# Up products of the second block's feed-forward by Strassen's scheme, with late roots of four norms and a final norm in two halves

## The chip, the cores and the metric

The kernel runs on one core of one Trainium2 chip. The metric is the device time of the whole program, 3941.75 us as the median of 3 runs (3941.59 to 3943.38). TensorE (PE) multiplies, VectorE (DVE) and ScalarE (ACT) do arithmetic on 128 partitions, GpSimd (POOL) so far only starts transfers, and SyncE (SP) loads the weights.

## The reference

Two blocks of two layers each work on 512 tokens of 1024 features. The first block is a gated linear attention layer and a latent attention layer, each with a convolutional feed-forward. The second block, twice over, is: a root-mean-square norm, three attentions side by side (a chunk band, a differential one, and one whose keys an indexer picks), a gated mix, a cross attention, and a SwiGLU feed-forward. A final norm ends it. What the change touches:

```python
def rmsnorm_2(x, g):
    x32 = x.astype(jnp.float32)
    y = x32 * lax.rsqrt(jnp.mean(x32 * x32, axis=-1, keepdims=True) + EPS)
    return y.astype(x.dtype) * g

# in each layer of the second block
h = rmsnorm_2(x, norm_mix)      # its first products: the indexer's queries and keys
...
h = rmsnorm_2(x, norm_ffn)
gate, up = split(h @ w_gu, 2)   # 1024 -> 2 x 2816
x = x + (silu(gate) * up) @ w_down
# after both layers
return rmsnorm_2(x, final_norm)
```

The last function stands here in short form. All is float32.

## The kernel before

Activations lie with features on the partitions: X is 8 tiles (k or n) of 128 features by tokens. Each float32 operand is split into a high part rounded to the matmul's 32-bit format (by ACT) and the rest (by DVE), and each product is three matmuls, high by high, high by low, low by high (mms3). MH and ML are the two parts of the normed activations, WH and WL those of a weight piece.

Weight pieces come in the order of one list through a ring of four slots (SP). Two pairs WH, WL take turns: piece k+1 is split while PE works on piece k, and the split waits until the products of piece k-1 are done. split_act and split_dve do this, and the code that calls them sets the place in each engine's queue. Every queue is in order, and semaphores join them.

The feed-forward of the second block (ffn_pe, swiglu_act, swiglu_dve, down_pe, down_act, down_dve; tags b0 and b1) goes over 22 column tiles j of the 2816 hidden features: j = 0 alone, then seven groups of three. A group has three up steps, each with a gate and a value product of 8 x 3 matmuls of 512 tokens. After a group's up steps come the down products of the group before, in two weight pieces (called D0 and D1 here) of four output tiles each. Between, ACT takes the silu of the gate, DVE multiplies by the value (called hidden here), and the result is split again into IH and IL (inter).

A norm (adaln, square_act, square_sum_dve, mean_pe, hr_act, hnorm_act, hnorm_dve) squares each finished tile of X on ACT, sums tiles 0 to 5 on DVE, and has PE multiply by a matrix of 1/1024 three times (the sum, tile 6 and tile 7), which leaves the mean on all partitions. ACT then makes the root by Ln and Exp, DVE scales each tile by root and gain, ACT rounds it to MH, DVE makes ML. The first product after a norm takes tile k as soon as it is there (first_mms3). Six such norms stand in the second block; the change touches those called "m" (before the indexer) and "f" (before the feed-forward) of both layers, and the final one.

Of the kernel before, what the change touches and what calls it, by code (L numbers as in the profile page):

```python
# [29 lines left out]
P = 128  # L30
# [80 lines left out]
def build(nc, io, counts):  # L111
    known = counts.known
    ctx = ExitStack()
    with ctx:
# [45 lines left out]
        conv = overlay("conv", [P, 2, 2, TOK], F32, 2 * HALF + 2 * inter_words)  # L160
        ps = ctx.enter_context(nc.psum_tensor("ps", [P, 8, BANK], F32))
# [29 lines left out]
        dve_done = ctx.enter_context(nc.semaphore("dve_done"))  # L191
        slot_loaded = [ctx.enter_context(nc.semaphore(f"slot_loaded_{i}")) for i in range(SLOTS)]
# [143 lines left out]
        splits = []  # L336
        for i, (key, parts, split) in enumerate(plan):
            loads[i % SLOTS] += 16 * len(parts)
            where[key] = (i, loads[i % SLOTS])
            if split:  # L340
                splits.append(key)
        split_at = {key: k for k, key in enumerate(splits)}

# [55 lines left out]

        def split_act(k):  # L400
# [3 lines left out]
            key = splits[k]  # L404
            i, n = where[key]
# [5 lines left out]
        def split_dve(k):  # L411
# [3 lines left out]
            key = splits[k]  # L415
            nc.vector.wait_ge(act_done, at(("rounded", k)))
# [17 lines left out]
        turn = [0]  # L434

        def take(key, bank=None):

            if bank is None:
                bank = turn[0] % 6
                turn[0] += 1  # L440
# [116 lines left out]
        def norm_buffers(spec):  # L557
            return late_tiles if spec[0] == "n0f" else (NF, NR)

        def residual_tiles(spec):  # L560
# [3 lines left out]
            if key == "n1":  # L564
                halves = (range(4), range(4, DT))
                return [(n, t0, tn) for (t0, tn), half in zip((ALL[0], ALL[1], ALL[1], ALL[0]), (0, 0, 1, 1)) for n in halves[half]]
            return [(n, t0, tn) for n in range(DT) for t0, tn in groups]

        def norm_tiles(groups):
            return [(k, t0, tn) for t0, tn in reversed(groups) for k in range(DT)]  # L570

# [12 lines left out]
        def square_act(spec, i):  # L584
# [4 lines left out]
            if i >= 2 and summed_squares(spec)[i - 1]:  # L589
                nc.scalar.wait_ge(dve_done, at(("hsq_summed", key, i - 1)))  # L590
# [7 lines left out]
        def square_sum_dve(spec, i):  # L598

            if i < 0 or not summed_squares(spec)[i]:  # L600
# [6 lines left out]

        def mean_pe(spec, i):
# [5 lines left out]
            n, t0, tn = tiles[i]  # L614
            bank = 7 if t0 else 6
            first = min(j for j in range(len(tiles)) if tiles[j][1] == t0 and own_product(spec, j))
            if i == first:
                take(("hms", key, t0), bank)
            if summed_squares(spec)[i]:
                nc.tensor.wait_ge(dve_done, at(("hsq_summed", key, i)))  # L620
            else:
                nc.tensor.wait_ge(act_done, at(("hsq", key, i)))
            m = nc.tensor.matmul(ps[:, bank, 0:tn], mat("mean1024"), NSQ[:, i % 2, 0:tn], start=(i == first), stop=(n == DT - 1))  # L623
            m.then_inc(pe_done, mark("pe", ("hsq_read", key, i), ("hms", key, t0)))
# [10 lines left out]
        def hnorm_act(spec, between=lambda i: None):  # L635
            key, groups, gains, shifts = spec
            for t0, tn in reversed(groups):
                hr_act(spec, t0, tn)
                for i, (k, u0, un) in enumerate(norm_tiles(groups)):
                    if u0 == t0:  # L640
                        nc.scalar.wait_ge(dve_done, at(("hscaled", key, i)))
                        nc.scalar.activation(hs(k, t0, tn, groups is MAIN)[0], norm_buffers(spec)[0][:, i % 3, 0:tn], ACT.Identity,
                                             bias=shifts(k, 0 if t0 else 1) if shifts else 0.0).then_inc(
                                                 act_done, mark("act", ("hh", key, i)))
                        between(i)

        GAINS = {"n0f": (0, 1), "n1": (1, 0), "n1f": (1, 1)}

        def hnorm_dve(spec, between=lambda i: None):
            key, groups, gains, shifts = spec  # L650
            tiles = norm_tiles(groups)
# [3 lines left out]
            def rest(i):  # L655
                k, t0, tn = tiles[i]
                nc.vector.wait_ge(act_done, at(("hh", key, i)))
                f = norm_buffers(spec)[0][:, i % 3, 0:tn]
# [8 lines left out]
            for i, (k, t0, tn) in enumerate(tiles):  # L667
# [7 lines left out]
                nc.vector.scalar_tensor_tensor(norm_buffers(spec)[0][:, i % 3, 0:tn], X[:, k, t0:t0 + tn], gains(k, 0 if t0 else 1),  # L675
                                               norm_buffers(spec)[1][:, t0:t0 + tn], ALU.mult, ALU.mult).then_inc(
                                                   dve_done, mark("dve", ("hscaled", key, i)))
# [94 lines left out]
        def residual_pe(key, act_in, groups, spec, chunks=None, passes=None):  # L772

            done = 0
            for name, tokens in passes or [(key, groups)]:
                for ck, n0, nn in chunks or [((name, i), 2 * i, 2) for i in range(DT // 2)]:
                    w = weights(ck)
                    kt = w.shape[1]
                    for j in range(nn):
                        for t0, tn in tokens:  # L780
# [4 lines left out]
                            if done > MEAN_LAG:  # L785
                                mean_pe(spec, done - 1 - MEAN_LAG)
# [2689 lines left out]
```

## Time and profile before

| what | value |
|---|---|
| median of 3 runs | 3941.75 us |
| profiled execution, its own time | 3945.47 us |
| its span | 3943.7 us |
| PE busy | 3759.4 us (95%) |
| DVE busy | 2040.9 us (52%) |
| ACT busy | 1423.2 us (36%) |
| POOL busy | 57.9 us (1%) |
| granted clock of TensorE, mean | 0.99 |

The span is what the trace covers, some 1.8 us less than the execution's time. A matmul's row has the time until its result is out; the next starts long before that, so the pace of PE is the distance from start to start. The first feed-forward of the second block runs from 2529 to 2893 us, the second from 3567 to 3931 us.

### The profile page before, as it was taken

Reading aid. Unit: us, or ns where it says so; the run is one execution under the profiler, and the core shown is the slowest. Engines: PE = TensorE matmul, PEld = TensorE weight load, DVE = VectorE, ACT = ScalarE, POOL = GpSimd, SP = SyncE. Lnnn points to the kernel's source line nnn. Section 1 sums busy time; section 2 is a strip of 40 time slices with the busy share of each in tenths; the row PEclk is TensorE's granted clock in tenths of the full one; section 3 lists DMA queues with packets and bytes.
Section 4 is the critical chain, followed back from the end, with each engine's and each line's share of the span. In section 5 each row is a group of like instructions: output and inputs, shape, how many; then the busy total and the mean of one; then the engine's idle time right before and its main releaser. Section 6 shows DMA issues by size and latency. Waiting matters only on the chain.

```text
span 3943.7 us, 48507 instructions
## 1 busy us (share of the span) xinstructions
PE 3759.4 (95%) x19650; PEld 2928.2 (74%) x19650; DVE 2040.9 (52%) x3190; ACT 1423.2 (36%) x2340; POOL 57.9 (1%) x115
## 2 busy tenths in 40 slices
PE   7998999999989899999999999899999999999998
PEld 6776888888855557887767677688876666867887
DVE  4553454454533326556786544443368765344334
ACT  4323332222344423333344443422234445433222
POOL 0000000000000000000000000000000000000000
PEclk9999999999999999999999999999999999999999
DMA  6321434233210012332322032233332222322331
GB/s 213 99 80 50 152 100 129 91 114 101 76 39 20 25 56 83 97 96 88 109 89 84 29 108 90 67 105 98 94 111 75 78 65 75 107 75 86 96 98 62
DMA packets 394091, 346.14 MB, mean 88 GB/s; under 512 B 11984, under 2 KB 355536, under 8 KB 393744
## 3 DMA queue, kind: packets, MB, share of 16 engines
q1 hardware_dynamic: 386912, 321.71, 26.8%
q0 software_dynamic: 6960, 21.34, 1.9%
q8 instruction: 158, 2.59, 0.3%
q14 instruction: 61, 0.50, 0.0%
HBM read 330.96 MB, written 2.10 MB: 84 GB/s over the span
## 4 chain that ended last, share of the span: by engine, by line
PE 78%; DVE 9%; ACT 4%; issue 2%; DMA 0%; POOL 0%; ACTq 0%; DVEq 0%
PE ps L455 51%; PE ps L466 4%; PE ps L468 4%; PE ps L467 4%; DVE WL L417 2%; PE ps L2384 1%; PE ps L2362 1%; PE ps L1971 1%; PE ps L1984 1%; ACT WH L409 1%; DVE arena_m L2635 1%; PE ps L695 1%; PE ps L623 1%; PE ps L696 1%; PE ps L697 1%
## 5 line engine op out<-in xcount | busy, mean ns | idle before, releaser
L417 DVE TENSOR_TENSOR WL<-ring,WH 128x2048 fp32r<-128x2048 f32 (+4 forms) x245 | 498.0, 2033 | 367.1 <-ACT WH L409 366.7
L409 ACT CAST WH<-ring 128x2048 fp32r<-128x2048 f32 (+4 forms) x245 | 415.5, 1696 | 431.6 <-PE ps L455 314.0
L455 PE MATMUL ps<-MH,WH 128*128 128x512 f32 (+1 forms) x1024 | 400.0, 391 | 8.1 <-DVE WL L417 8.1
L455 PE MATMUL ps<-ML,WH 128*128 128x512 f32 (+1 forms) x1024 | 399.8, 390 | 0.0
L455 PE MATMUL ps<-MH,WL 128*128 128x512 f32 (+1 forms) x1024 | 399.8, 390 | 0.0
L455 PE MATMUL ps<-IH,WH 128*128 128x512 f32 (+1 forms) x880 | 327.7, 372 | 7.7 <-DVE modv L756 3.2
L455 PE MATMUL ps<-IL,WH 128*128 128x512 f32 (+1 forms) x880 | 324.9, 369 | 0.0
L455 PE MATMUL ps<-IH,WL 128*128 128x512 f32 (+1 forms) x880 | 324.2, 368 | 0.0
L466 PE MATMUL ps<-MH,WH 128*128 128x512 f32 x768 | 321.6, 419 | 0.0
L468 PE MATMUL ps<-MH,WL 128*128 128x512 f32 x768 | 301.4, 392 | 0.0
L467 PE MATMUL ps<-ML,WH 128*128 128x512 f32 x768 | 300.2, 391 | 0.0
L455 PE MATMUL ps<-HH,WH 128*128 128x512 f32 (+1 forms) x728 | 247.3, 340 | 1.4 <-DVE WL L417 1.4
L455 PE MATMUL ps<-HL,WH 128*128 128x512 f32 (+1 forms) x728 | 245.5, 337 | 0.0
L455 PE MATMUL ps<-HH,WL 128*128 128x512 f32 (+1 forms) x728 | 245.0, 336 | 0.0
L455 PEld LDWEIGHTS ps<-MH,WH 128*128 128x128 f32 (+1 forms) x1024 | 192.3, 188 | 50.8 <-DVE WL L417 9.8
L455 PEld LDWEIGHTS ps<-MH,WL 128*128 128x128 f32 (+1 forms) x1024 | 192.2, 188 | 41.2
L455 PEld LDWEIGHTS ps<-ML,WH 128*128 128x128 f32 (+1 forms) x1024 | 192.1, 188 | 40.7
L1596 ACT ACTIVATE conv<-ps,vec 128x512 f32<-128x512 f32 (+1 forms) x132 | 92.4, 706 | 322.8 <-PE ps L455 322.1
L1616 DVE SCALAR_TENSOR_TENSOR conv<-ps,vec,conv 128x511 f32<-128x511 f32 (+1 forms) x132 | 86.9, 658 | 216.2 <-ACT conv L1596 215.7
L455 PEld LDWEIGHTS ps<-IH,WH 128*128 128x128 f32 x880 | 166.3, 189 | 39.4 <-DVE WL L417 4.4
L466 PEld LDWEIGHTS ps<-MH,WH 128*128 128x128 f32 x768 | 144.5, 188 | 60.3 <-DVE arena_m L2016 9.7
L455 PEld LDWEIGHTS ps<-IH,WL 128*128 128x128 f32 x880 | 166.2, 189 | 28.2
(338 smaller groups left out, 6782.8 us busy)
## 6 DMA issues: line engine op xcount, KB each, us to landing
ring<-in_w_in SPq DMA_DIRECT2D x62, 1024.0 KB, 5.2
ring<-in_w_ada SPq DMA_DIRECT2D x48, 1024.0 KB, 8.0
ring<-in_ffn_w_up SPq DMA_DIRECT2D x88, 512.0 KB, 5.1
ring<-in_w_gu SPq DMA_DIRECT2D x88, 512.0 KB, 5.0
ring<-in_ffn_w_down SPq DMA_DIRECT2D x28, 768.0 KB, 4.8
ring<-in_w_down SPq DMA_DIRECT2D x28, 768.0 KB, 4.4
ring<-in_gla_w_in SPq DMA_DIRECT2D x24, 512.0 KB, 3.9
arena_m<-arena_m POOLq DMA_DIRECT2D x72, 128.0 KB, 2.9
```

Of the source, the lines that this page charges most:

```text
L409: nc.scalar.copy(split_slot(key, WH), raw_slot(key)).then_inc(act_done, mark("act", ("rounded", k)))
L417: nc.vector.tensor_tensor(split_slot(key, WL), raw_slot(key), split_slot(key, WH).bitcast(F32), ALU.subtract).then_inc(dve_done, mark("dve ...
L455: m = nc.tensor.matmul(out, l, r, start=(i == 0), stop=(i == len(pairs) - 1))
L466: nc.tensor.matmul(out, lh, rh, start=first and i == 0, stop=False)
L467: nc.tensor.matmul(out, lh, rl, start=False, stop=False)
L468: m = nc.tensor.matmul(out, ll, rh, start=False, stop=end)
L623: m = nc.tensor.matmul(ps[:, bank, 0:tn], mat("mean1024"), NSQ[:, i % 2, 0:tn], start=(i == first), stop=(n == DT - 1))
L695: nc.tensor.matmul(out, wh, xh, start=(k == 0), stop=False)
L696: nc.tensor.matmul(out, wl, xh, start=False, stop=False)
L697: m = nc.tensor.matmul(out, wh, xl, start=False, stop=(k == DT - 1))
L1596: nc.scalar.activation(conv[:, j % 2, part, t0:t0 + tn], bank_of(key)[:, 0:tn], ACT.Identity, scale=v("conv_w", 132 * l + 44 + t), bias=v( ...
L1616: nc.vector.scalar_tensor_tensor(cv[:, t0 + 1:t0 + tn], u[:, 0:tn - 1], v("conv_w", 132 * l + t), cv[:, t0 + 1:t0 + tn], ALU.mult, ALU.add ...
```

## The change

**Seven products for eight.** For the column tiles j = 4 to 21 of b0 and b1, the up step (K = 1024, 256 output columns, 512 tokens) is cut into 2 x 2 blocks: K in halves of 4 tiles, columns in gate and value, tokens in halves of 256. Seven products p1 to p7 of 4 x 3 matmuls of 256 tokens stand for the 48 matmuls of 512. The weight blocks are four parts of the slot (a11, a12, a22, and s1 in place of a21) and three sums s2, s3, s4, which GpSimd makes. Each of the seven is split on its own ("chunk"), in two turns of the pair WH, WL. The token sums are made once per layer (XF, split into TH and TL). The results are put together on ACT (p1, p5, p7 copied from PSUM), GpSimd (u4, u3, c22) and DVE (q, c11, c12, c21).

**Late roots.** Before the norms m and f, the first product runs on x times gain, not yet times the root; its result is multiplied by the root afterwards (raw_scaled_dve). The normed tiles are still made, for the next products. The sums of squares move from DVE to GpSimd.

**Final norm in halves.** The last four output tiles of the last down step are made for tokens 256 to 511 first, then for 0 to 255; root, scaling and store go by halves.

```diff
+        def seven(key):
+            return key[0] == "up" and key[1][0] == "b" and key[2] >= FIRST_SEVEN
...
+        CHUNKS = (("a11", "s2", "s1", "s3"), ("a12", "s4", "a22"))
...
+        def chunk_act(k, c):
...
+            if last[0] == "seven" and c < len(CHUNKS[last[2]]):
+                nc.scalar.wait_ge(pe_done, at(("chunk_used", k - SPLITS, c)))
+            else:
+                nc.scalar.wait_ge(pe_done, at(("split_used", k - SPLITS)))
...
+            nc.scalar.copy(chunk_place(k, c, WH), chunk_source(key, name)).then_inc(
+                act_done, mark("act", ("chunk_rounded", k, c)))
...
+        def combine_pool(key, name, before):
+            out, a, b, op = {"s3": ("s3", "a11", "a21", ALU.subtract), "s1": ("s1", "a21", "a22", ALU.add),
+                             "s2": ("s2", "s1", "a11", ALU.subtract), "s4": ("s4", "a12", "s2", ALU.subtract)}[name]
...
+            if before and name != "s1":
+                nc.gpsimd.wait_ge(dve_done, at(("chunk_of", before, name)))
...
+        def raw_mms3(spec, tiles):
+            key = spec[0]
+            for k in range(DT):
+                nc.tensor.wait_ge(dve_done, at(("raw_low", key, k)))
+                for out, w, t0, tn in tiles:
...
+                if k < RAW_MEANS:
+                    mean_pe(spec, DT - RAW_MEANS + k)
...
         def hnorm_dve(spec, between=lambda i: None):
             key, groups, gains, shifts = spec
+            if raw(spec):
+                split_dve(after(first_piece(spec)))
...
+                    if spec[0][0] == "m" and i == 4:
+                        split_dve(after(("idx", spec[0][1], 1)))
...
+        PRODUCTS = [("p1", 0, 0, "a", FIRST_HALF, (MH, ML), 0, FIRST_HALF), ("p6", 0, 1, "a", SECOND_HALF, (TH, TL), QUARTER, SECOND_HALF),
+                    ("p5", 0, 2, "b", FIRST_HALF, (TH, TL), 0, FIRST_HALF), ("p7", 0, 3, "b", SECOND_HALF, (TH, TL), 0, SECOND_HALF),
+                    ("p2", 1, 0, "c", FIRST_HALF, (MH, ML), QUARTER, FIRST_HALF), ("p3", 1, 1, "c", SECOND_HALF, (MH, ML), QUARTER, SECOND_HALF),
+                    ("p4", 1, 2, "d", FIRST_HALF, (TH, TL), QUARTER, FIRST_HALF)]
...
+        def seven_dve(tag, j):
...
+            nc.vector.wait_ge(pe_done, at(("p3", tag, j)))
+            add_bank(gate[:, FIRST_HALF], "c", FIRST_HALF, gate[:, FIRST_HALF], "c11")
+            nc.vector.wait_ge(pool_done, at(("u4", tag, j)))
+            add_bank(gate[:, SECOND_HALF], "c", SECOND_HALF, gate[:, SECOND_HALF], "c12", ("free", ("seven", tag, j, "c")))
+            if nxt:
+                chunk_dve(nxt + 1, 1)
+            else:
+                split_dve(after(key))
...
+        def combined_low_dve(tag, part):
+            ks = slice(QUARTER * part, QUARTER * part + QUARTER)
+            nc.vector.wait_ge(act_done, at(("combined_high", tag, part)))
+            nc.vector.tensor_tensor(TL[:, ks, :], XF[:, ks, :], TH[:, ks, :].bitcast(F32), ALU.subtract).then_inc(
+                dve_done, mark("dve", ("combined_low", tag, part)))
...
+            combined_inputs_pool(tag)
+            combine(0)
+            combine(1)
+            for n, key in enumerate(keys):
...
+                for name, dst, a, b in (("u4", gate[:, SECOND_HALF], q, value[:, SECOND_HALF]),
+                                        ("u3", value[:, FIRST_HALF], value[:, FIRST_HALF], q),
+                                        ("c22", value[:, SECOND_HALF], value[:, SECOND_HALF], value[:, FIRST_HALF])):
...
+                combine(n + 2)
...
+            if spec[0] == "final" and g == GROUPS - 1:
+                tiles = residual_tiles(spec)
+                return [(tiles[k][0] // 4, [(n % 4, t0, tn) for n, t0, tn in tiles[k:k + 4]]) for k in range(0, 12, 4)]
...
-            nc.vector.wait_ge(act_done, at(("hr", "final", CTX)))
-            for k in range(DT):
+        def final_dve(half, ks):
+            t0, tn = FINAL_HALVES[half]
+            for k in ks:
+                nc.vector.wait_ge(act_done, at(("hr", "final", t0)))
```

DVE's queue at the last up step of a group in b0 and the down step behind it, before (conv holds gate and value):

```order
L417 TENSOR_TENSOR WL<-ring,WH 128x1536 [waits act_done]
L1649 TENSOR_TENSOR conv<-ps,conv 128x512 [waits act_done,pe_done]
L1582 TENSOR_TENSOR IL<-conv,IH 128x512 [waits act_done]
L417 TENSOR_TENSOR WL<-ring,WH 128x1536 [waits act_done]
L1672 TENSOR_TENSOR X<-ps,X 128x512 [waits dve_done,pe_done] x4
```

The same place of the changed kernel (TB holds gate and value; q, c11, c12, then the split, then c21):

```order
L1835 TENSOR_TENSOR TB<-ps,TB 128x256 [waits act_done]
L1835 TENSOR_TENSOR TB<-ps,TB 128x256 [waits pe_done]
L1835 TENSOR_TENSOR TB<-ps,TB 128x256 [waits pool_done]
L502 TENSOR_TENSOR WL<-ring,WH 128x1536 [waits act_done]
L1835 TENSOR_TENSOR TB<-ps,TB 128x256 [waits pool_done,pe_done]
L1863 TENSOR_TENSOR TB<-TB 128x512 [waits dve_done,act_done]
L1940 TENSOR_TENSOR ILB<-TB,IHB 128x512 [waits act_done]
L502 TENSOR_TENSOR WL<-ring,WH 128x1536 [waits act_done]
L2057 TENSOR_TENSOR X<-ps,X 128x512 [waits dve_done,pe_done] x4
```

The split of D0 stood first, and waited for ACT alone; now it stands behind c11 and c12, of which the first waits for p3, the last product but one of the step.

DVE's queue in b0 from the normed tile 7 to the down step of j = 0, in the changed kernel (L761 multiplies by the root, L2023 and L2028 are hidden, L1889 the rest of the token sums):

```order
L835 TENSOR_TENSOR ML<-XF,MH 128x512 [waits act_done] x2
L761 TENSOR_TENSOR TB<-ps,spare 128x512 [waits pe_done] x2
L2023 TENSOR_TENSOR TB<-TB 128x512 [waits act_done,dve_done]
L1940 TENSOR_TENSOR ILB<-TB,IHB 128x512 [waits act_done]
L502 TENSOR_TENSOR WL<-ring,WH 128x2048 [waits act_done]
L2028 TENSOR_TENSOR TB<-ps,TB 128x512 [waits act_done,pe_done]
L1940 TENSOR_TENSOR ILB<-TB,IHB 128x512 [waits act_done]
L502 TENSOR_TENSOR WL<-ring,WH 128x2048 [waits act_done]
L2028 TENSOR_TENSOR TB<-ps,TB 128x512 [waits act_done,pe_done]
L1940 TENSOR_TENSOR ILB<-TB,IHB 128x512 [waits act_done]
L1889 TENSOR_TENSOR TL<-XF,TH 128x2048 [waits act_done]
L502 TENSOR_TENSOR WL<-ring,WH 128x512 [waits act_done]
```

Before, the split for j = 1 stood where the two L761 stand; it has moved ahead of the normed tiles. L761 and L1889 were not there.

GpSimd's queue in the changed kernel behind the token sums, where before there was nothing (the four sums of one weight piece, the three additions of one step, the next sums):

```order
L474 TENSOR_TENSOR SB<-ring 128x512 [waits dve_done,slot_loaded_1]
L474 TENSOR_TENSOR ring<-ring 128x4x128 [waits pool_done]
L474 TENSOR_TENSOR SB<-ring 128x512 [waits dve_done,pool_done]
L474 TENSOR_TENSOR SB<-ring,SB 128x512 [waits dve_done,pool_done]
L1914 TENSOR_TENSOR TB<-TB 128x256 [waits dve_done,act_done]
L1914 TENSOR_TENSOR TB<-TB 128x256
L1914 TENSOR_TENSOR TB<-TB 128x256 [waits pool_done]
L474 TENSOR_TENSOR SB<-ring 128x512 [waits dve_done,slot_loaded_2]
```

The sums for a piece two steps ahead stand behind the additions of the present step, and wait for the split of the piece between.

## Rows read from the trace of the kernel before

**Rows 1.** The page: span, busy time, and the chain's shares by engine.
```profile
span 3943.7 us, 48507 instructions
PE 3759.4 (95%) x19650; PEld 2928.2 (74%) x19650; DVE 2040.9 (52%) x3190; ACT 1423.2 (36%) x2340; POOL 57.9 (1%) x115
PE 78%; DVE 9%; ACT 4%; issue 2%; DMA 0%; POOL 0%; ACTq 0%; DVEq 0%
```

**Rows 2.** Stretches: length, busy of PE, PEld, DVE, ACT, POOL, clock, DMA.
```profile
1852.99:1890.03 37.04, 33.34 (x127) 24.10 (x125) 18.55 (x21) 14.88 (x21) 6.64 (x13) 0.91 0.59 174
2528.00:2534.50 6.50, 5.05 (x12) 4.01 (x13) 6.47 (x11) 3.74 (x6) 0.00 (x0) 0.50 0.06 22
2575.57:2583.09 7.52, 5.94 (x26) 4.24 (x24) 6.63 (x9) 4.55 (x4) 0.00 (x0) 1.00 0.33 105
2632.20:2664.84 32.64, 32.64 (x145) 27.04 (x144) 9.80 (x8) 8.13 (x8) 0.00 (x0) 1.00 0.36 98
2664.84:2681.16 16.32, 16.32 (x73) 13.52 (x72) 9.91 (x11) 3.91 (x3) 0.00 (x0) 1.00 0.29 95
2893.33:2929.13 35.80, 32.10 (x127) 23.24 (x125) 18.50 (x21) 14.82 (x21) 6.64 (x13) 0.95 0.62 180
```

**Rows 3.** Timeline of PE: first of 36 matmuls of 256 tokens, and what follows.
```profile
1051.02 0.28 PE L455 MATMUL ps<-IH,WH 128*128 128x256 f32 x1
...
1055.33 0.40 PE L455 MATMUL ps<-IH,WH 128*128 128x512 f32 x1
```

**Rows 4.** Groups by line and shape, 2529 to 2893 us: busy, mean ns, idle.
```profile
L417 DVE TENSOR_TENSOR WL<-ring,WH 128x1536 fp32r<-128x1536 f32 x14 | 24.6, 1758 | 9.9 <-ACT WH L409 9.9
L409 ACT CAST WH<-ring 128x1536 fp32r<-128x1536 f32 x14 | 20.7, 1475 | 12.1 <-PE ps L455 12.1
L417 DVE TENSOR_TENSOR WL<-ring,WH 128x2048 fp32r<-128x2048 f32 x21 | 48.1, 2291 | 22.5 <-ACT WH L409 22.5
L409 ACT CAST WH<-ring 128x2048 fp32r<-128x2048 f32 x22 | 41.9, 1903 | 60.2 <-PE ps L455 60.2
L417 DVE TENSOR_TENSOR WL<-ring,WH 128x512 fp32r<-128x512 f32 x2 | 1.4, 684 | 0.0
L409 ACT CAST WH<-ring 128x512 fp32r<-128x512 f32 x2 | 1.2, 615 | 0.0
```

**Rows 5.** Groups by line and shape, whole span: PSUM operands of 256 columns.
```profile
L2003 DVE TENSOR_TENSOR arena_m<-ps,arena_m 128x256 f32<-128x256 f32 x16 | 6.7, 421 | 0.3
L2035 ACT COPY arena_m<-ps 128x256 f32<-128x256 f32 x16 | 6.0, 373 | 28.9 <-PE ps L1971 28.9
```

**Rows 6.** Timeline at norm f of b0: start, us, engine, line, idle before.
```profile
2522.82 2.92 PE L623 MATMUL ps<-spare,mats 128*128 128x512 f32 x6
...
2525.79 0.69 ACT L630 ACTIVATE stage_b<-ps,eps 128x512 f32<-128x512 f32 x1 [1.22 <-PE ps L623]
...
2527.17 1.41 DVE L675 SCALAR_TENSOR_TENSOR stage_b<-X,vec,stage_b 128x512 f32<-128x512 f32 x2 [3.45 <-ACT stage_b L633]
...
2529.45 0.76 PE L695 MATMUL ps<-MH,WH 128*128 128x512 f32 x1 [3.70 <-DVE ML L664]
...
2536.21 1.47 DVE L664 TENSOR_TENSOR ML<-stage_b,MH 128x512 fp32r<-128x512 f32 x2
```

**Rows 7.** Timeline of the end: last means, final scaling, stores.
```profile
3930.80 2.92 PE L623 MATMUL ps<-spare,mats 128*128 128x512 f32 x6
...
3935.14 5.39 DVE L3252 SCALAR_TENSOR_TENSOR stage_b<-X,vec,stage_b 128x512 f32<-128x512 f32 x8 [3.45 <-ACT stage_b L633]
3936.59 4.31 SPq L3308 DMA_DIRECT2D out<-stage_b  x4
```

**Rows 8.** GpSimd's costliest group by line.
```profile
L2084 POOL DMA_DIRECT2D arena_m<-arena_m x80 | 38.9, 494 | 281.8 <-ACT arena_m L2040 238.1 <-DVE arena_m L2095 23.5 <-ACT arena_m L2575 7.6
```

**Rows 9.** Timeline of DVE: one split of 1024 columns.
```profile
3435.88 1.22 DVE L417 TENSOR_TENSOR WL<-ring,WH 128x1024 fp32r<-128x1024 f32 x1
```

More of the change, by code:

```diff
@@ L339, in build @@
             where[key] = (i, loads[i % SLOTS])
-            if split:
+            if seven(key):
+                for part in (0, 1):
+                    where["seven", key, part] = where[key]
+                    splits.append(("seven", key, part))
+            elif split:
                 splits.append(key)
         split_at = {key: k for k, key in enumerate(splits)}
+        for key in list(split_at):
+            if key[0] == "seven":
+                split_at[key[1]] = split_at["seven", key[1], 1]
         def after(key):
@@ L404, in split_act @@
             key = splits[k]
+            if key[0] == "seven":
+                for c in range(len(CHUNKS[key[2]])):
+                    chunk_act(k, c)
+                return
             i, n = where[key]
@@ L415, in split_dve @@
             key = splits[k]
+            if key[0] == "seven":
+                for c in range(len(CHUNKS[key[2]])):
+                    chunk_dve(k, c)
+                return
             nc.vector.wait_ge(act_done, at(("rounded", k)))
@@ L1517, in up_pe @@
             for j in group(g):
+                if seven(("up", tag, j)):
+                    seven_pe(tag, j)
+                    continue
                 w = split_weights(("up", tag, j))
-                if j == 0:
+                if j == 0 and raw(spec):
+                    tiles = [(take(("up", tag, j, part, CTX)), lambda k, part=part: two(w, k, 128 * part, 128 * part + 128), CTX, SEQ)
+                             for part in range(2)]
+                    raw_mms3(spec, tiles).then_inc(pe_done, mark("pe", ("raw_read", spec[0], DT - 1), ("up", tag, j, 0, CTX),
+                                                                 ("up", tag, j, 1, CTX), split_used(("up", tag, j))))
+                elif j == (1 if raw(spec) else 0):
                     for t0, tn in reversed(groups):
@@ L1547, in down_pe @@
                     out = take(("down", tag, g, 4 * i + n, t0))[:, 0:tn]
[L1548 to L1550 removed]
+                    m = mms3(out, [(two(w, k, 128 * n, 128 * n + 128), inter(tag, g, k, t0, t0 + tn)) for k in range(len(group(g)))])
                     m.then_inc(pe_done, mark("pe", ("down", tag, g, 4 * i + n, t0), ("down", tag, g),
@@ new lines, in seven_pe @@
+        def seven_pe(tag, j):
+            key = ("up", tag, j)
+            if j == FIRST_SEVEN:
+                nc.tensor.wait_ge(dve_done, at(("combined_low", tag, 1)))
+            for name, half, c, bank, part, (xh, xl), k0, tokens in PRODUCTS:
+                k = split_at["seven", key, half]
+                if part is FIRST_HALF:
+                    take(("seven", tag, j, bank))
+                out = bank_of(("seven", tag, j, bank))[:, part]
+                nc.tensor.wait_ge(dve_done, at(("chunk", k, c)))
+                wh, wl = chunk_place(k, c, WH), chunk_place(k, c, WL)
+                for i in range(QUARTER):
+                    nc.tensor.matmul(out, wh[:, i], xh[:, k0 + i, tokens], start=i == 0, stop=False)
+                    nc.tensor.matmul(out, wh[:, i], xl[:, k0 + i, tokens], start=False, stop=False)
+                    m = nc.tensor.matmul(out, wl[:, i], xh[:, k0 + i, tokens], start=False, stop=i == QUARTER - 1)
+                m.then_inc(pe_done, mark("pe", (name, tag, j), ("chunk_used", k, c), ("split_used", k)))
```

393 lines of the change are left out of this document (322 added, 71 removed).

## The prediction

> **What bounds the kernel now.** I read the page first, then stretches of the second block's feed-forward, then the timeline at the norms. PE is busy 95% of the span and carries 78% of the chain; DVE is at 52%, ACT at 36%, GpSimd at 1% [rows 1]. In a steady group the three up steps are 144 matmuls of 512 tokens in 32.64 us, the down step 72 in 16.32 us, both 0.2267 us apart with no gap, while DVE is busy 9.8 us of the 32.64 [rows 2]. So here only PE's pace counts. At a norm it is a chain: the last means start at 2522.82, the root takes until 2527.17, PE waits 3.70 us and starts again at 2529.45 [rows 6], and from 2528.0 to 2534.5 the granted clock is 0.50, the lower of its two levels (1.2 GHz), after that idle time [rows 2].
>
> **Fewer products.** Matmuls of 256 tokens run 36 in 4.31 us (1051.02 to 1055.33), 0.1197 us apart, each with a weight load of its own [rows 3]. That is 5.6% more than half of 0.2267, so not all of the eighth is gained. An up step goes from 48 x 0.2267 = 10.88 us to 84 x 0.1197 = 10.05 us, one product being 1.44 us: 0.83 us, times 18 steps, times 2 layers, **29.7 us less** if PE never waits.
>
> **What the seven products ask of the others.** Per up step DVE has seven chunk splits of 0.68 us [rows 4], four additions from PSUM of 0.42 us [rows 5], and hidden and inter of about 0.69: 7.9 us of 10.05. ACT has seven casts of 0.62 [rows 4], three copies of 0.37 [rows 5], silu and rounding of about 0.6 each: 6.7 us. Chunks for the next step follow the product that frees their place by one to three us, and PE needs them a whole step later, so in the first two steps of a group I see no wait. GpSimd does four sums of 512 columns and three of 256. No row shows it computing (it issues transfers, 0.49 us each) [rows 8]. From below I take DVE's time for the same shape, 0.68, from above DVE's for four times the columns, 2.29 [rows 4]: 4.0 to about 14 us per step. At the upper end GpSimd itself would bound the step. I take the lower half, near DVE's own time and under 1 us, and its sums then fit: they stand two steps ahead.
>
> **The last step of a group.** PE goes on with D0, whose weights DVE must have split. That split stood ahead of the step's work; now it stands behind c11, which waits for p3. Product p3 ends 8.62 us into the step, its result is out 0.2 us later, c11 and c12 take 0.35 us each from start to start, the split takes 1.76 [rows 4], and PE starts 0.15 us after it: 11.4 us, where p4 has ended at 10.05. PE waits 1.35 us in each group, six groups, two layers: **16.2 us more**. Behind the split wait c21, hidden, inter and the split of D1, and D1 is needed 8 us later: no second wait. The idle time is short; a like one of 1.5 us stands in 2575.57 to 2583.09, at full clock [rows 2].
>
> **Norm m (twice).** From the last down product the way to the end of the indexer's two pieces and the next 48 products took 37.04 us in the first layer and 35.80 in the second [rows 2]. Now the raw products start at once: 10.88 us and 2.6 us for three means, of which the third ends 6.65 us in. The root takes 1.6 us more, and the eight normed tiles go from 8.2 us at 1.27 us each (10.5 us from 2527.17 to 2537.68) [rows 6]. In their midst stands a split of 2048 columns, 1.90 us on ACT and 2.29 on DVE [rows 4], which puts the last tile at 22.4 us. PE, ready for the second piece at 13.5, takes tile after tile and ends it at 23.1 instead of 18.9; with 48 products, 34.0. **3.0 and 1.8 us less.**
>
> **Norm f (twice).** From the last product of the cross attention's output to the start of j = 4 it took 60.27 us (2522.82 to 2583.09) [rows 2, 6]. Now: 13.46 us of raw products and means, 10.88 for j = 1. DVE is through with the normed tiles at 18.75 us; then come two multiplications by the root, silu, hidden, rounding, inter, and the split for j = 2 ends at 25.8: PE waits 1.5 us. With j = 2 and 3 PE is at 47.6. At j = 3 DVE splits half of the token sums (1.90 us on ACT, 2.29 on DVE) [rows 4] ahead of the split of the second down piece, which is ready 6.7 us after the step instead of at 2.7; PE waits 4.0 us, and the first chunk comes behind four additions: 57.6. An idle time as long as the 3.70 us of before lets the clock fall. At norm m of the second layer 35.80 us [rows 2] less the 6.63 from last means to start [rows 6] leave 29.2 us for 120 matmuls, which at 0.2267 take 27.2: a fall costs 2.0 us. 59.6 against 60.27: **0.7 us less each.** The early idle time and clock are saved, and paid again 45 us later.
>
> **Final norm.** Half products cost 72 x 0.1197 - 36 x 0.2267 = 0.46 us, and five more means of half width 2.1 us ahead of the last product. Behind it the root and eight scalings are half as wide (8 x 0.67 = 5.39 us before) [rows 7], but DVE scales the first half in between, which puts the last addition back by 1.5 us. I make it 13.4 us from the old 3930.80, where it was 12.9: **0.5 us more**, give or take 1.5.
>
> **Sum.** 29.7 - 16.2 + 4.8 + 1.4 - 0.5 = 19.2 us. The profiled execution took 3945.47 us, 3.7 over the median of the runs: 3926.3 in such an execution, **3923 us** as the median, 0.5% less. Its own range is 3908 to 3937: GpSimd's sums and the waits at the norms may shift it by some 15 us either way.
>
> **Rivals.**
> First, slower: GpSimd and DVE hold each other up. Nothing in the trace shows the two computing at once [rows 8]. If no operation of GpSimd runs beside one of DVE with both inputs in SBUF, then the first two steps of a group have 21 splits and the like of DVE (14.4 us) and nine sums and six additions of GpSimd in one line. At DVE's own speed that is 8.7 us, 23.1 in all in 20.1 us and a slack of nearly 4: nothing happens. At half DVE's speed (1.22 us, the row of 1024 columns) [rows 9] it is 15.1 us and the middle step's inter ends 9.7 us into the last step instead of 4. ACT's cast for D0 stands behind it and ends at 11.3, DVE's split at 13.1: PE waits 3.2 us, not 1.35, and every second time the clock falls, 2.0 us. That is 12 x 4.2 = 50 us against 29.7. At norm f the token sums, four of 1024 columns at 2.29 us, would stand between hidden, inter and the split for j = 2: 4.0 us and a fallen clock more, in each layer. In all 27 us slower, **3969 us**. It decides from about 1 us per sum of 512 columns on. The Trainium skill states this lock (SBUF — State Buffer, section Who interferes with whom: a VectorE instruction with two SBUF inputs and a GpSimd instruction that reads SBUF block each other for the whole instruction). It also gives 4497 ns for a GpSimd addition of 2048 columns (GPSIMD Engine Reference, section 3.1), an estimate of 1.12 us for 512; with that and the lock the sum would come out near 3946, no gain. No run so far shows either.
>
> Second, better: DVE and ACT are quicker through these chains than I make them, GpSimd costs nothing, and the waits for D0 shrink to 0.7 us (8 us in all), those at f to half (4 us more): **3908 us**; without any such wait 3900.
>
> Third, the change does not do what it says: with a weight load for every 256 tokens instead of 512 PE's pace is that of the loads (84 instead of 48 per step). Loads take 0.19 us (27.04 for 144) but overlap [rows 2]; in 36 in a row they did not slow the pace [rows 3]. Were it 0.130 in the long run, a step would take 10.92 us and the 29.7 would be lost: **3953 us**.
>
> **Chances.** Forecast 0.48; GpSimd and DVE in each other's way 0.30, of which a third is the mild form near 3946; quicker chains 0.16; pace of loads 0.06. What a measurement of this kernel can tell from no change is about 0.2%, 8 us. Faster: the forecast but for its upper end, and the second rival, 0.61. Within 0.2%: the mild lock and small pieces of the others, 0.12. Slower: 0.27. The range from 3900 to 3972 leaves out the far ends of the first and second rival.
>
> **What would show it.** Right: L455-like rows of 256 tokens 0.120 us apart; PE idle some 1.1 to 1.4 us before each D0, released by DVE's split of 1536 columns, twelve times; no idle time between the cross attention's output and the raw products; 1.5 us before j = 2 and about 4 before the second down piece of j = 0, released by DVE. Wrong: DVE's splits of 512 columns at much over 0.69 us, or long idle times of DVE ended by GpSimd; GpSimd's sums over 1 us; waits for D0 over 3 us with the clock at 0.50 behind them; GpSimd busy through the whole up steps; or any wait of PE for a chunk.

## The result and the profile after

The changed kernel takes 3961.99 us as the median of 5 runs, against 3941.75 before: ratio 1.0047 (1.0036 to 1.0058), slower by 20.2 us by the medians (18.5 by the ratio), where 19 less was forecast. It lies 7 us below the first rival's 3969. The profiled execution took 3966.62 us, 21.1 more than that of before.

The page of the changed kernel, answering [rows 1]:

```profile
span 3964.8 us, 52752 instructions
PE 3748.3 (95%) x20992; PEld 2979.3 (75%) x20992; DVE 2314.5 (58%) x3586; ACT 1551.6 (39%) x2702; POOL 441.7 (11%) x395
PE 69%; DVE 15%; ACT 5%; issue 4%; POOL 0%; DMA 0%; ACTq 0%; DVEq 0%; POOLq 0%
L541 PE MATMUL ps<-IHB,WH 128*128 128x512 f32 (+1 forms) x364 | 146.0, 401 | 33.0 <-DVE WL L502 33.0
```

PE computes 11 us less than before, but DVE's share of the chain has grown from 9% to 15%: in front of the high-by-high down products (IHB, the rounded half of inter) PE stood idle 33.0 us, always released by DVE's split of a weight piece.

Stretches of the changed kernel, answering [rows 2]: norm m of the first layer, norm f, three up steps and the down step behind them, twice, and norm m of the second layer. Columns are length, then busy time of PE, PEld, DVE, ACT, POOL, the granted clock, DMA.

```profile
1854.01:1888.54 34.53, 31.72 (x126) 22.66 (x127) 20.63 (x26) 15.45 (x21) 7.76 (x14) 0.95 0.59 163
2521.09:2584.19 63.10, 55.09 (x225) 43.24 (x223) 41.86 (x44) 27.79 (x36) 18.58 (x9) 0.95 0.30 84
2638.11:2670.48 32.37, 30.40 (x254) 30.22 (x252) 28.67 (x34) 16.39 (x32) 23.56 (x18) 1.00 0.31 90
2670.48:2688.53 18.05, 18.05 (x72) 14.72 (x73) 10.60 (x15) 4.18 (x6) 4.21 (x4) 0.91 0.36 103
2688.53:2720.90 32.37, 30.39 (x253) 30.21 (x252) 28.68 (x34) 16.39 (x32) 23.56 (x18) 1.00 0.32 90
2720.90:2737.34 16.44, 16.44 (x72) 13.59 (x73) 10.50 (x15) 4.18 (x6) 4.22 (x4) 1.00 0.40 113
2901.65:2936.32 34.67, 31.86 (x126) 22.69 (x126) 20.55 (x26) 15.45 (x21) 7.73 (x14) 0.95 0.58 163
```

PE's work in three up steps fell from 32.64 to 30.4 us (forecast 30.15). But 2 us of idle time stand behind it, and of the two down steps one ran 1.6 us longer than the other, at a mean clock of 0.91. A group takes 50.42 or 48.81 us, where it took 48.96. DVE, busy 9.8 us of three up steps before, is now busy 28.7.

GpSimd's groups over the whole span, and DVE's in the up steps of the first layer, answering [rows 4, 5, 8]; the second number behind the bar is the mean in ns:

```profile
L1914 POOL TENSOR_TENSOR TB<-TB 128x256 f32<-128x256 f32 x108 | 117.9, 1106 | 77.4 <-ACT TB L1800 62.2 <-DVE TB L1835 11.3 <-ACT WH L451 1.0
L474 POOL TENSOR_TENSOR SB<-ring 128x512 f32<-128x512 f32 x72 | 102.1, 1418 | 183.3 <-DVE WL L459 173.5 <-DMA ring<-in_w_gu 6.9
L1877 POOL TENSOR_TENSOR XF<-XF 128x1024 f32<-128x1024 f32 x8 | 24.2, 3031 | 36.5 <-DVE ML L835 36.0
```

```profile
L459 DVE TENSOR_TENSOR WL<-SB,WH 128x512 fp32r<-128x512 f32 x54 | 54.2, 1004 | 5.9 <-ACT WH L451 5.9
L1835 DVE TENSOR_TENSOR TB<-ps,TB 128x256 f32<-128x256 f32 x72 | 28.7, 414 | 9.0 <-POOL TB L1914 5.7 <-PE ps L1784 3.0
L1863 DVE TENSOR_TENSOR TB<-TB 128x512 f32<-128x512 f32 x17 | 23.7, 1393 | 0.5
```

A GpSimd sum of 512 columns takes 1.42 us, where I had taken less than 1. DVE's split of 512 columns takes 1.00 us instead of 0.68, hidden (L1863) 1.39 instead of the 0.69 that I had taken. Only the addition with an operand in PSUM is as short as it was, 0.41.

The last step of a group in the changed kernel, timeline of GpSimd, ACT, DVE and PE; its first product starts at 2658.27:

```profile
2659.74 1.29 POOL L474 TENSOR_TENSOR SB<-ring 128x512 f32<-128x512 f32 x1
...
2663.20 1.78 DVE L1863 TENSOR_TENSOR TB<-TB 128x512 f32<-128x512 f32 x1
2664.51 1.62 POOL L474 TENSOR_TENSOR SB<-ring,SB 128x512 f32<-128x512 f32 x1
2665.07 0.62 ACT L1933 CAST IHB<-TB 128x512 fp32r<-128x512 f32 x1 [4.05 <-DVE TB L1863]
2665.72 0.97 DVE L1940 TENSOR_TENSOR ILB<-TB,IHB 128x512 fp32r<-128x512 f32 x1 [0.74 <-ACT IHB L1933]
2666.39 1.50 ACT L490 CAST WH<-ring 128x1536 fp32r<-128x1536 f32 x1
2667.16 3.64 POOL L1914 TENSOR_TENSOR TB<-TB 128x256 f32<-128x256 f32 x3 [1.03 <-DVE TB L1835]
2667.94 0.42 DVE L1835 TENSOR_TENSOR TB<-ps,TB 128x256 f32<-128x256 f32 x1 [0.41 <-POOL TB L1914]
2668.28 1.93 DVE L502 TENSOR_TENSOR WL<-ring,WH 128x1536 fp32r<-128x1536 f32 x1
...
2670.48 0.47 PE L541 MATMUL ps<-IHB,WH 128*128 128x512 f32 x1 [1.97 <-DVE WL L502]
```

Hidden of the middle step ends only at 2664.98, 6.7 us into the last. ACT has waited 4.05 us for it with the rounding at the head of its queue; D0's cast stands behind that and ends at 2667.89, DVE's split at 2670.21. (The delay against PE's pace is 0.16 us more than the idle time shown.) Two things stand ahead of that split, the cast and c12, and c12 starts only 0.05 us after the cast's end, because it waited 0.41 us for GpSimd's u4. But u4 had itself waited for DVE's q, which stands in DVE's queue behind the same late inter. Otherwise a late result of GpSimd holds up little: over the groups of the first layer DVE waited 5.7 us in all for GpSimd, only in the last steps, and ACT 2.8 us, once, in the first group.

The last group of the first layer in the same kernel; its last step starts at 2856.71:

```profile
2854.64 3.57 POOL L1914 TENSOR_TENSOR TB<-TB 128x256 f32<-128x256 f32 x3 [2.00 <-ACT TB L1800]
2858.20 0.68 DVE L459 TENSOR_TENSOR WL<-SB,WH 128x512 fp32r<-128x512 f32 x1
...
2860.10 0.69 DVE L1863 TENSOR_TENSOR TB<-TB 128x512 f32<-128x512 f32 x1
...
2863.39 2.25 POOL L1914 TENSOR_TENSOR TB<-TB 128x256 f32<-128x256 f32 x3 [5.18 <-ACT TB L1800]
...
2868.23 0.47 PE L541 MATMUL ps<-IHB,WH 128*128 128x512 f32 x1 [1.28 <-DVE WL L502]
```

Here no piece is left to make sums for, so GpSimd does the three additions of the middle step and then nothing until the next three; the order of DVE's queue is the same as in the other groups. DVE's operations take their own time again, hidden of the middle step ends 4.1 us into the last step instead of 6.7, and the delay is 1.44 us, not 2.13 (forecast 1.35); so it is in the second layer. With the same queues and the same additions, what makes the difference inside this one kernel is the four sums that GpSimd does beside DVE behind the middle step's additions.

Norm f of the first layer in the changed kernel:

```profile
2540.41 12.36 POOL L1877 TENSOR_TENSOR XF<-XF 128x1024 f32<-128x1024 f32 x4 [18.01 <-DVE ML L835]
...
2541.70 1.66 DVE L2023 TENSOR_TENSOR TB<-TB 128x512 f32<-128x512 f32 x1 [0.17 <-ACT TB L1998]
2544.05 2.13 DVE L1940 TENSOR_TENSOR ILB<-TB,IHB 128x512 fp32r<-128x512 f32 x1 [0.69 <-ACT IHB L1933]
2546.10 4.42 DVE L502 TENSOR_TENSOR WL<-ring,WH 128x2048 fp32r<-128x2048 f32 x1
...
2550.58 0.80 PE L541 MATMUL ps<-MH,WH 128*128 128x512 f32 x1 [4.48 <-DVE WL L502]
```

During GpSimd's token sums each operation of DVE is one to two microseconds longer than alone, the split for j = 2 4.42 instead of 2.29, and PE waits 4.48 us where I had 1.5.

### The profile page after: what moved, and what is told of

It is laid out like the page before. It is cut to its first block, busy times and chain, and to the rows that moved or that the text cites. A ratio compares the mean times of both kernels' runs of the same rounds, so it can differ in the third digit from the quotient of the medians.

```text
span 3964.8 us, 52752 instructions
## 1 busy us (share of the span) xinstructions
PE 3748.3 (95%) x20992; PEld 2979.3 (75%) x20992; DVE 2314.5 (58%) x3586; ACT 1551.6 (39%) x2702; POOL 441.7 (11%) x395
## 4 chain that ended last, share of the span: by engine, by line
PE 69%; DVE 15%; ACT 5%; issue 4%; POOL 0%; DMA 0%; ACTq 0%; DVEq 0%; POOLq 0%
PE ps L541 39%; PE ps L552 4%; PE ps L554 4%; PE ps L553 4%; DVE WL L502 3%; DVE WL L459 2%; PE ps L2798 1%; ACT WH L490 1%; PE ps L2776 1%; PE ps L2385 1%; PE ps L1782 1%; PE ps L1784 1%; PE ps L1783 1%; PE ps L2398 1%; DVE TB L1863 1%
## 5 line engine op out<-in xcount | busy, mean ns | idle before, releaser
L552 PE MATMUL ps<-MH,WH 128*128 128x512 f32 x768 | 322.0, 419 | 0.0
L541 PE MATMUL ps<-IH,WH 128*128 128x512 f32 (+1 forms) x528 | 190.5, 361 | 7.6 <-DVE modv L929 3.2
L541 PE MATMUL ps<-IL,WH 128*128 128x512 f32 (+1 forms) x528 | 188.0, 356 | 0.0
L541 PE MATMUL ps<-IH,WL 128*128 128x512 f32 (+1 forms) x528 | 187.2, 355 | 0.0
L541 PE MATMUL ps<-IHB,WH 128*128 128x512 f32 (+1 forms) x364 | 146.0, 401 | 33.0 <-DVE WL L502 33.0
L541 PE MATMUL ps<-MH,WH 128*128 128x512 f32 x400 | 159.0, 398 | 13.9 <-DVE WL L502 13.9
L554 PEld LDWEIGHTS ps<-MH,WL 128*128 128x128 f32 x768 | 144.7, 188 | 32.1
L553 PEld LDWEIGHTS ps<-ML,WH 128*128 128x128 f32 x768 | 145.3, 189 | 27.0 <-issue 2.4
L1782 PE MATMUL ps<-TH,WH 128*128 128x256 f32 x576 | 163.0, 283 | 0.0
L1783 PE MATMUL ps<-TL,WH 128*128 128x256 f32 x576 | 163.0, 283 | 0.0
L1784 PE MATMUL ps<-TH,WL 128*128 128x256 f32 x576 | 163.0, 283 | 0.0
```

The source lines that it names most:

```text
L541: m = nc.tensor.matmul(out, l, r, start=(i == 0), stop=(i == len(pairs) - 1))
L552: nc.tensor.matmul(out, lh, rh, start=first and i == 0, stop=False)
L553: nc.tensor.matmul(out, lh, rl, start=False, stop=False)
L554: m = nc.tensor.matmul(out, ll, rh, start=False, stop=end)
L1782: nc.tensor.matmul(out, wh[:, i], xh[:, k0 + i, tokens], start=i == 0, stop=False)
L1783: nc.tensor.matmul(out, wh[:, i], xl[:, k0 + i, tokens], start=False, stop=False)
```

## The experiments

**Without GpSimd's arithmetic.** All of seven_pool is left out, and the waits for it; the splits read the slot's own parts.

```diff
-            nc.vector.wait_ge(pool_done, at(("u4", tag, j)))
...
-            nc.vector.wait_ge(pool_done, at(("c22", tag, j)))
...
-                seven_pool(f"b{l}")
```

> Left out: all of GpSimd's arithmetic for the seven products (token sums, the four weight sums, u4, u3, c22); the splits read unsummed parts of the slot, so the output is not the reference's. TensorE, ACT and DVE do as many operations as in the changed kernel. Theory (GpSimd's additions and DVE's two-input operations hold each other up): the terms of the prediction come out, 1.4 us before each D0, about 1.5 us before j = 2 in norm f, DVE's splits of 512 columns at 0.68 us throughout; 3923 us. Rival 1 (GpSimd is only slow, and its results come late): also 3923. Rival 2 (the order of DVE's queue alone makes the waits, whatever GpSimd does): waits of 2.1 us and the clock's falls stay, 3955.

Measured: 3932.64 us, 0.9971 (0.9961 to 0.9982), 11 us faster than before. (Each ratio is to the kernel before as it ran beside that experiment, here 3944.97 us.) The split of 512 columns, and the last step of the same group as in the first of the timelines above (the second group of the first layer), whose first product starts at 2651.71:

```profile
L457 DVE TENSOR_TENSOR WL<-ring,WH 128x512 fp32r<-128x512 f32 x122 | 81.3, 690 | 24.1 <-ACT WH L449 23.3
```

```profile
2654.60 0.69 DVE L1936 TENSOR_TENSOR ILB<-TB,IHB 128x512 fp32r<-128x512 f32 x1 [0.74 <-ACT IHB L1929]
2655.25 0.42 DVE L1833 TENSOR_TENSOR TB<-ps,TB 128x256 f32<-128x256 f32 x1
2660.55 0.76 DVE L1833 TENSOR_TENSOR TB<-ps,TB 128x256 f32<-128x256 f32 x2 [4.87 <-PE ps L1782]
2661.22 1.75 DVE L500 TENSOR_TENSOR WL<-ring,WH 128x1536 fp32r<-128x1536 f32 x1
```

The middle step's inter ends 3.6 us into the last step instead of 8.4, DVE idles 4.87 us until p3, and the chain c11, c12, split is the one I had worked out: eleven delays of 1.44 us and one of 1.54 (forecast 1.35), and no fall of the clock behind them. So rival 2, the order alone, falls. That it is 11 and not 18 us faster is answered under the table below.

**GpSimd at work, nobody waiting.** As many additions of the same shapes, on tiles of GpSimd's own; each waits for the one before, and both inputs are one and the same tile. One of the changed lines:

```diff
-            nc.gpsimd.tensor_tensor(chunk_source(key, out), chunk_source(key, a), chunk_source(key, b), op).then_inc(
+            nc.gpsimd.tensor_tensor(SB[:, 0], mats[:, 0:4], mats[:, 0:4], ALU.subtract).then_inc(
```

> As the one without GpSimd's arithmetic, but GpSimd does as many additions of the same shapes at the same points of its queue, on tiles of its own, and nobody waits for them; the output is not the reference's. Theory (the two engines hold each other up): DVE's splits of 512 columns take 1.0 to 1.8 us beside GpSimd again, the wait before D0 is near 1.9 us, and the time is 3948 to 3960. Rival 1 (late results of GpSimd): nobody waits for them, so 3923, as without them.

Measured: 3939.2 us, 0.999 (0.9981 to 0.9999): between the two theories, and the number I had written was missed. Against the kernel without GpSimd's work it loses in norm f (60.98 and 64.54 us, there 59.66 and 59.87), nothing in the groups. The load was also lighter than the real one: DVE's splits took 0.86 us on the mean, GpSimd's additions of 256 columns 0.79 instead of 1.11; why, stays open. Hidden of the middle step ends 3.6 us into the last step here, sooner than in the group without sums above (4.1), so D0 is not held up. So this run shows the price of a lighter load, and does not test the groups under the real one.

**The two engines by themselves.** DVE, GpSimd and ACT repeat one operation each; every pair of phases differs in who else is at work.

> A program of its own, without the reference's computation: DVE, GpSimd and ACT repeat one operation, first each alone, then two engines at once, with every operand in SBUF but where PSUM is named. Theory (DVE and GpSimd exclude each other while each reads two SBUF operands): side by side, a DVE subtraction of 512 columns takes its own time and up to that of one addition of GpSimd, 1.2 to 2.0 us, where GpSimd is at work, and the same with one operand in PSUM, or with ACT beside GpSimd, takes what it takes alone. Rival (the engines share the bandwidth of SBUF): every pair of engines stretches by a like factor, ACT beside GpSimd too.

Measured (one run), groups by line in stretches of one phase each: DVE with two SBUF operands alone, then beside GpSimd; DVE with one operand in PSUM beside GpSimd; DVE with a single SBUF operand alone, then beside GpSimd; ACT beside GpSimd; GpSimd alone.

```profile
L152 DVE TENSOR_TENSOR dc<-da,db 128x512 f32<-128x512 f32 x23 | 15.9, 692 | 0.8
L152 DVE TENSOR_TENSOR dc<-da,db 128x512 f32<-128x512 f32 x10 | 16.3, 1632 | 0.3
L155 POOL TENSOR_TENSOR pc<-pa,pb 128x512 f32<-128x512 f32 x10 | 15.9, 1588 | 0.8
L158 DVE TENSOR_TENSOR dc<-ps,da 128x512 f32<-128x512 f32 x18 | 12.4, 691 | 0.6
L161 DVE TENSOR_SCALAR dc<-da 128x512 f32<-128x512 f32 x9 | 3.8, 427 | 0.3
L161 DVE TENSOR_SCALAR dc<-da 128x512 f32<-128x512 f32 x9 | 12.3, 1367 | 0.3
L167 ACT COPY ab<-aa 128x512 f32<-128x512 f32 x23 | 14.2, 618 | 246.8 <-DVE dc L164 246.1
L155 POOL TENSOR_TENSOR pc<-pa,pb 128x512 f32<-128x512 f32 x12 | 15.1, 1262 | 22.0 <-DVE dc L152 21.1
```

Beside each other the two take turns, ten operations of each in 16 us: DVE 1.63 us instead of 0.69, GpSimd 1.59 instead of 1.26. A pair so takes 0.3 us less than the two alone, one after the other (1.95). With an operand in PSUM DVE is untouched, and so is ACT (0.618 us beside GpSimd and beside DVE). Shared bandwidth falls; the engines exclude each other. The Trainium skill's rule (SBUF — State Buffer, section Who interferes with whom), that one of the two blocks for the other's whole instruction, agrees with these rows but for that 0.3 us.

**D0's split ahead of the middle step's inter.** On ACT and on DVE, in the last step of each group; the core of the edit:

```diff
...
             keep("p1", "a", FIRST_HALF, gate[:, FIRST_HALF])
+            if not nxt:
+                split_act(after(key))
+                round_inter_act(tag, j - 1, CTX)
...
+            if not nxt:
+                split_dve(after(key))
+                rest_inter_dve(tag, j - 1, CTX)
```

> In the last up step of each group the cast and the split of D0 stand ahead of the rounding of the step before, on ACT and on DVE; nothing else moves. Theory (the locked work of DVE makes the inter of the middle step late, ACT's cast of D0 stands behind it, DVE's split behind that): the wait before D0 and the clock's fall behind it go, 12 x 2.1 and some 7 x 1.6 us, about 3926. Rival (DVE has no room left in these steps, and the wait turns up before D1 or before the next chunks instead): 3948 to 3958.

Measured: 3930.28 us, 0.9967 (0.9954 to 0.9979). Of the delays before D0 only that in the first group of each layer is left (1.94 and 0.84 us); the groups up to the last down steps take 265.17 and 264.13 us instead of 284.04 and 283.07. GpSimd does the same sums and additions as before: the order frees PE of the stretched DVE.

**Norm f mended.** GpSimd's token sums wait for the split of j = 2, and both halves of the token sums are rounded and split at j = 2.

```diff
-            nc.gpsimd.wait_ge(dve_done, at(("hnormed", key)))
+            nc.gpsimd.wait_ge(dve_done, at(("split", split_at["up", tag, 2])))
...
-                if j in (2, 3):
-                    combined_low_dve(tag, j - 2)
+                if j == 2:
+                    combined_low_dve(tag, 0)
+                    combined_low_dve(tag, 1)
```

> Norm f alone is mended: GpSimd's token sums wait until DVE has split the weights of j = 2, and both halves of the token sums are rounded and split at j = 2. Theory (the token sums on GpSimd stretch hidden, inter and the split of j = 2, and the second half stands in the way of D1's split): the waits of 4.5 and 3.4 us go and the clock's falls behind them; norm f 55 to 57 us instead of 63.1 and 64.7, about 3946. Rival (DVE needs this time anyway, and the first chunks come late instead): 3954 to 3962.

Measured: 3945.27 us, 1.0004 (0.9995 to 1.0013). Norm f takes 54.09 and 56.48 us instead of 63.10 and 64.74; the two waits fall to 1.12 us before j = 2 and under 0.3 before D1, and nothing came late in their place but the first product of the seven in the second layer (2.3 us). The waits before D0 are as they were, but for the first group of the second layer (2.13 us instead of 3.25).

**Which queue holds D0.** Norm f mended, and DVE's split of D0 alone moved ahead of c11.

```diff
+            if not nxt:
+                split_dve(after(key))
             nc.vector.wait_ge(pe_done, at(("p3", tag, j)))
```

> Norm f mended; in the last step of a group only DVE's split of D0 moves, from behind c11 and c12 to ahead of c11; ACT's cast of D0 and the inter of the middle step stay where they are. If the wait of DVE for p3 and u4 is what holds D0 (the prediction's reason): PE's idle time before D0 falls from 1.97 to 0.5 us or less, no clock falls, about 3918. If ACT's cast is late, because it stands behind the rounding of the middle step, which waits for DVE: the cast ends 9.6 us into the step, DVE's split at 11.5, PE's idle time is 1.3 to 1.5, without the clock's falls 3925 to 3930.

Measured: 3943.92 us, 1.0004 (0.9995 to 1.0013), the same as with the norm mended alone. A last step, whose first product starts at 2650.00:

```profile
2656.80 0.62 ACT L1933 CAST IHB<-TB 128x512 fp32r<-128x512 f32 x1 [4.05 <-DVE TB L1863]
...
2658.12 1.49 ACT L490 CAST WH<-ring 128x1536 fp32r<-128x1536 f32 x1
...
2658.90 3.64 POOL L1914 TENSOR_TENSOR TB<-TB 128x256 f32<-128x256 f32 x3 [1.03 <-DVE TB L1835]
2659.65 2.31 DVE L502 TENSOR_TENSOR WL<-ring,WH 128x1536 fp32r<-128x1536 f32 x1 [0.89 <-ACT WH L490]
```

DVE now stands idle 0.89 us and waits for ACT's cast; then its split meets GpSimd's three additions and takes 2.31 us, where it took 1.93 behind c12. PE's idle time is 1.97 as before. So, with the sums at work, taking away the wait for p3 and u4 alone gains nothing: ACT's cast is just as late, as the expectation's second half had it; it had not counted that the split would meet the additions. In the last group of each layer, which has no sums behind the middle step, the same move takes the delay from 1.44 us to nothing: there the expectation's first half holds, and with it the prediction's reason.

**The sums on DVE, D0 left late.** Norm f mended, GpSimd's arithmetic on DVE.

```diff
...
-            nc.gpsimd.tensor_tensor(chunk_source(key, out), chunk_source(key, a), chunk_source(key, b), op).then_inc(
+            nc.vector.tensor_tensor(chunk_source(key, out), chunk_source(key, a), chunk_source(key, b), op).then_inc(
```

> Norm f mended, D0's split left where the change puts it, and all of GpSimd's arithmetic for the seven products on DVE. Theory (GpSimd's additions stretch DVE, so the inter of the middle step, ACT's cast of D0 and DVE's split of it come late): with DVE alone the wait before D0 falls to the predicted 1.3 to 1.4 us, no clock falls behind it, and the time is 3919 to 3926, against 3943 with GpSimd. Rival (the amount of work on DVE makes the inter late, on whichever engine the sums stand): DVE has 3.5 us more per step, waits of 2 us and more, 3943 to 3960.

Measured: 3955.28 us, 1.0029 (1.0017 to 1.0040). The rival was right. DVE's splits are 0.68 us again, yet PE's idle time before D0 is 2.47 to 2.51 us in the steady groups of the first layer: the middle step's inter ends 9.2 us into the last step. What counts is how long DVE is taken up ahead of it, by its own work or by GpSimd's.

**The three additions alone on DVE.** The weight sums stay on GpSimd.

> Norm f mended, D0's split left where the change puts it; u4, u3 and c22 stand on DVE, the four weight sums stay on GpSimd. If the late u4 of GpSimd is what keeps c12 and with it D0's split: waits of 1.4 us and 3920 to 3928. If the weight sums beside the splits are what makes the middle step's inter late: waits near 1.8 to 2.0 us stay, 3936 to 3945.

Measured: 3971.0 us, 1.0073 (1.0059 to 1.0086), worse than either number. Idle time before D0 is 3.5 to 3.7 us with a fall of the clock behind each, but for the last group of each layer (1.74 us, no fall). DVE has both the additions and GpSimd's weight sums beside them in line. As DVE got more work by it, this run alone does not clear u4; the last group of the changed kernel does, where u4 comes from GpSimd too and nothing is late.

**Late roots and final norm alone.** Every up step with its 48 matmuls (FIRST_SEVEN = 22, seven_pool left out).

> Late roots and the halved final norm alone, every up step with its 48 matmuls. By the changed kernel's trace: norms m 2.5 and 1.1 us less, final norm 0.8 more, and norm f without token sums 54 instead of 60.3 us: 3927. If the late roots of norm f cost time by themselves (the raw product, the split moved ahead, the two multiplications by the root): 3942 to 3948.

Measured: 3937.69 us against 3944.97, 0.9986 (0.9977 to 0.9994): faster, but by half of what I had written. Norm f takes 55.57 and 55.56 us, norm m 34.55 and 35.48, and the last two down steps with the end take 0.8 us longer. By the marks of the table below these stages give 10.9 us in the profiled execution; the medians differ by 7.3.

**Both moves together**, and the same with the sums on DVE.

> The split of D0 moved ahead and norm f mended, both together. If the two waits are independent: 3929 less 16, 3913. If one of them hides the other: 3920 to 3929.

> As the one with both, but all of GpSimd's arithmetic for the seven products (token sums, weight sums, u4, u3, c22) stands on DVE. DVE's own work grows to 11.4 us per up step and some 43 us of a group's 46.6. If what stretches DVE is GpSimd: its splits are 0.68 us throughout, it catches up in the down step, and the time is that of both or a little less, 3908 to 3914. Rival (DVE in one line is late for the chunks of the next step): waits of PE in the up steps, 3925 to 3940.

Measured: 3909.77 us, 0.9917 (0.9903 to 0.9930), and 3908.75 us, 0.9913 (0.9899 to 0.9926), against 3943.48. Both beat the kernel before by 0.8% and cannot be told apart. The gains add up. A norm f, three up steps and a down step with both moves, GpSimd at work:

```profile
2520.08:2574.20 54.12, 52.75 (x225) 41.54 (x223) 42.83 (x44) 27.85 (x35) 22.47 (x9) 1.00 0.33 94
2625.65:2655.89 30.24, 30.24 (x254) 30.23 (x253) 27.64 (x32) 15.86 (x31) 21.87 (x17) 1.00 0.33 96
2655.89:2672.23 16.34, 16.34 (x74) 13.52 (x73) 11.50 (x18) 4.82 (x7) 5.79 (x6) 1.00 0.38 113
```

A steady group takes 46.6 us instead of 48.96, with no wait and at full clock, though DVE is still busy 27.6 of 30.2 us.

## Why the prediction was wrong

The table cuts the profiled executions at PE's own marks, in us; where a stage stands in both layers the two are added for the changes.

| stage | before | after | forecast | change | without GpSimd |
|---|---|---|---|---|---|
| norm m | 37.04, 35.80 | 34.53, 34.67 | -4.8 | -3.6 | -3.6 |
| norm f | 60.26, 60.39 | 63.10, 64.74 | -1.4 | +7.2 | -1.1 |
| j = 4 to the last two down steps | 277.60, 277.58 | 284.04, 283.07 | -13.5 | +11.9 | -10.4 |
| last two down steps of b0 | 32.65 | 33.43 | 0 | +0.8 | +0.8 |
| the same of b1, and the end | 45.55 | 46.46 | +0.5 | +0.9 | +0.9 |
| code that is the same in both | 3116.83 | 3120.76 | 0 | +3.9 | +4.6 |

Of the last row 0.75 us is time that PE lost ahead of the first raw product of norm m in the first layer; the +0.8 of the last two down steps of b0 is nearly all the same loss in the second layer. The forecast had nothing there. What else the last row shows is no effect of the change that could be told from chance: the row lies between 3112.7 and 3121.4 us in the executions told of here. Without GpSimd's work 8.8 us are gained where 19.2 were forecast, and of the 10.4 between them it makes 4.6; 3.1 are missing in the groups, and the rest in small terms.

- **Fewer products**: right. 84 matmuls in 10.08 us (forecast 10.05), 28.8 us in all instead of 29.7; the pace is not that of the weight loads, so the third rival falls.
- **"I take the lower half, near DVE's own time and under 1 us, and its sums then fit"**: the step that failed. It put GpSimd's sums too low, and what they cost DVE at nothing. The sum of 512 columns takes 1.26 us alone and 1.42 or more in the changed kernel, and beside it DVE's split of 512 columns takes 1.00 us on the mean instead of 0.68, up to 1.8. So the middle step's inter ends 8.4 us into the last step, not the 4 that the prediction reckoned with. The rival had named the place (the middle step's inter late, ACT's cast of D0 behind it) and the point, about 1 us per sum, from which it decides. I had given it 0.30. Its 3969 comes near with its terms somewhat too high: 50 us at D0 against 40 measured, and 10.6 more at norm f than before against 7.2.
- **D0's wait**: its chain was right where GpSimd is idle, 1.44 us against 1.35. In the changed kernel the late inter decides, except in the last group of each layer. Delays of 2.13 us, 4.78 and 3.25 in the first group of each layer and 1.44 in the last, are 28.0 us, and falls of the clock behind 7 of the 12, at some 1.6 us each, 11 more. By the table it is 40.7 us instead of 16.2 (the 28.8 that the products give and the 11.9 by which the two stages still are longer).
- **Norm f**: the forecast's 59.6 is met without GpSimd's work (59.66 and 59.87), and its terms are near too: the waits before j = 2 and D1 are 1.14 and 3.46 us there (forecast 1.5 and 4.0), with a fall of the clock behind the second. With it the token sums stretch hidden, inter and the split of j = 2, as the rival had it, to a wait of 4.48 us; that of D1 is 3.45 here.
- **Norm m and the end**: the right sign, 1.2 us less gain and 0.4 more loss than forecast, not counting the time ahead of the first raw product.
- The estimate of 1.12 us per sum, worked out from the Trainium skill's figure (GPSIMD Engine Reference, section 3.1), was nearer to the 1.26 measured than mine; I gave its rule little weight because no row of before showed the two engines at once.

## What to carry to other kernels

Work handed to GpSimd beside a DVE whose operands lie in SBUF is not free: count both engines' time in one line (here less some 0.3 us a pair), unless one operand of DVE comes from PSUM. Where an engine runs nearly full, look not at its share but at what stands behind its latest result in the in-order queues of others: here one cast on ACT behind a rounding that nobody needed yet, with the split behind it, cost some 40 us where Strassen's scheme gave 28.8. Put what PE needs next ahead of what it needs two steps later; that was worth 32 us with GpSimd's work unchanged.

## What the runs showed that was not expected

- DVE's tensor_scalar is also held up, with its single operand in SBUF: 0.427 us alone, 1.367 beside GpSimd, while an addition from PSUM stays at 0.691.
- Idle time of 1.97 us before D0 was followed by a stretch at the lower of the two clock levels in five of eight cases of the changed kernel, idle time of 1.28 to 1.38 us in none of the twelve without GpSimd's work. Why three of the eight stayed at full clock is open. A lateness of 0.7 us so cost up to 2.3.
- The same sums on GpSimd or on DVE cost the same once the order no longer hangs on them (0.9917 and 0.9913), though DVE's splits take 0.98 to 1.00 us in the one and 0.68 in the other.
